# Four feed forwards: the fourth-quarter sums of the crossed norm moved behind VectorE's second plain multiplication, and T2 kept in the norm's own row

## What is computed

```python
def swiglu(h, w_in, w_out):
    g, u = jnp.split(h @ w_in, 2, axis=-1)
    return (jax.nn.silu(g) * u) @ w_out

h = h + g2 * swiglu(modulate(h, norm2_g[l], sh2, sc2), ffn_w_in[l], ffn_w_out[l])   # first block
x = layer_norm(ALPHA * x + g_f * swiglu_2(h, ffn_w1[i], ffn_w3[i], ffn_w2[i]), ...)  # second block
```

## Time and profile before

| | before |
|---|---|
| median of three runs | 4000.85 us |
| the profiled execution, its own time | 4003.02 us |
| its span, first to last instruction | 4000.9 us |
| TensorE matmuls busy | 3700.5 us (92%) |
| VectorE, ScalarE, GpSimd busy | 2337.9, 1505.0, 1802.7 us |
| mean granted TensorE clock | 0.947 of full speed |

### The profile page before, as it was taken

One profiled execution on the slowest core, in us unless ns is written; L12 is line 12 of the kernel. 1 busy time (PEld: TensorE's weight loads), 2 busy tenths in 40 slices (PEclk: granted clock), 3 DMA queues, 4 the chain that ended last, 5 costly groups with the idle time before them and its releaser, 6 DMA issues. The chain is left out here.

```text
span 4000.9 us, 82113 instructions
## 1 busy us (share of the span) xinstructions
PE 3700.5 (92%) x33646; PEld 3242.0 (81%) x33646; DVE 2337.9 (58%) x4324; ACT 1505.0 (38%) x2826; POOL 1802.7 (45%) x1226
## 2 busy tenths in 40 slices
PE   6998899999899899989799999979999999988997
PEld 5877799999677788868698888769999878668996
DVE  3345566666553766685557775276666640637665
ACT  3235333333365443332234443243333241644443
POOL 2201455554344777632233432155555332737884
PEclk8999999999999999989879999889999989989998
DMA  4223233332201444432201100223333211012331
GB/s 177 69 98 106 90 101 112 119 108 95 70 5 48 152 154 154 137 112 109 76 20 31 29 21 25 80 85 106 106 116 114 72 63 64 23 54 74 101 101 63
DMA packets 159555, 343.99 MB, mean 86 GB/s; under 512 B 33487, under 2 KB 89295, under 8 KB 158799
## 3 DMA queue, kind: packets, MB, share of 16 engines
q1 hardware_dynamic: 139311, 266.37, 20.2%
q10 hardware_dynamic: 19872, 72.36, 5.3%
HBM read 323.88 MB, written 16.93 MB: 85 GB/s over the span
## 5 line engine op out<-in xcount | busy, mean ns | idle before, releaser
L1450 POOL TENSOR_TENSOR feed_low<-feed_sums,feed_high 128x512 fp32r<-128x512 f32 x320 | 502.0, 1587 | 476.0 <-ACT feed_high L1444 468.0
L1450 POOL TENSOR_TENSOR feed_low<-ring,feed_high 128x512 fp32r<-128x512 f32 x448 | 596.2, 1347 | 193.6 <-ACT feed_high L1444 96.7
L1444 ACT ACTIVATE feed_high<-ring 128x512 fp32r<-128x512 f32 x448 | 278.5, 626 | 433.2 <-PE ps L1692 243.2
L1676 PE MATMUL ps<-hn_high,feed_high 128*128 128x384 f32 (+1 forms) x1280 | 401.9, 314 | 0.8 <-ACT feed_gate L1764 0.8
L1677 PE MATMUL ps<-hn_low,feed_high 128*128 128x384 f32 (+1 forms) x1280 | 395.4, 309 | 0.0
L1678 PE MATMUL ps<-hn_high,feed_low 128*128 128x384 f32 (+1 forms) x1280 | 395.3, 309 | 0.0
L1690 PE MATMUL ps<-feed_hid,feed_high 128*128 128x384 f32 (+1 forms) x1056 | 378.8, 359 | 13.6 <-DVE h L1874 6.1
L1691 PE MATMUL ps<-feed_hid,feed_high 128*128 128x384 f32 (+1 forms) x1056 | 375.9, 356 | 0.0
L1692 PE MATMUL ps<-feed_hid,feed_low 128*128 128x384 f32 (+1 forms) x1056 | 375.5, 356 | 0.0
L1444 ACT ACTIVATE feed_high<-feed_sums 128x512 fp32r<-128x512 f32 x320 | 189.3, 626 | 488.5 <-DVE feed_sums L1469 275.0
L1676 PE MATMUL ps<-cross_high,feed_high 128*128 128x384 f32 (+1 forms) x960 | 300.3, 313 | 22.7 <-issue 21.7
(11 more groups left out here) (639 smaller groups left out, 9489.1 us busy)
## 6 DMA issues: line engine op xcount, KB each, us to landing
feed_side_ring<-in_ada ACTq DMA_DIRECT2D x138, 512.0 KB, 4.3
ring<-in_ffn_g SPq DMA_DIRECT2D x88, 512.0 KB, 4.9
ring<-in_ffn_u SPq DMA_DIRECT2D x88, 512.0 KB, 3.7
ring<-in_ffn_d SPq DMA_DIRECT2D x88, 512.0 KB, 3.8
diff_side_ring<-in_ada SPq DMA_DIRECT2D x32, 512.0 KB, 4.2
ring<-in_od_in SPq DMA_DIRECT2D x24, 512.0 KB, 4.0
ring<-in_ev_in SPq DMA_DIRECT2D x23, 512.0 KB, 5.2
ring<-in_even_in SPq DMA_DIRECT2D x20, 512.0 KB, 4.1
```

The lines of the kernel that those rows point to most:

```text
L1444: act.activation(self.high[:, e % self.SLOTS, :], self.source(name, n), ACT.Copy).then_inc(self.high_ready, 1)
L1450: pool.tensor_tensor(self.low[:, slot, :], self.source(name, n), self.high[:, slot, :].bitcast(F32), ALU.subtract).then_inc(self.low_ready, 1)
L1676: pe.matmul(dst, high, vh, start=c == 0, stop=False)
```

## The change

In `cross`, T2 is written in place into the second half of its `norm_sq` row in place of `cross_raw`, and `crossed` now counts with T2. For c = 0 and 2 VectorE first waits for GpSimd's low part of norm row c + 4. The two drains behind T2 are gone. The four fourth-quarter sums are a method of their own, `add_fourth`; VectorE calls them after `plain_multiply(1)`, which has moved ahead of `put_low(0)`. They count in a new semaphore. `high_cross` and `low_cross` are two instructions each, one for T1 and T3, one for T2. On ScalarE, `high_fourth` waits for the four sums and stands, with `put_hidden(0)` behind it, after `first_copy` of chunk 2; `put_hidden(0)` now also waits for all four `cross_low`. A wait of ScalarE for a22 of chunk 1 is gone.

```diff
@@ class CrossedStream, cross @@
-        t1, t2, t3 = (self.k.cross_raw[:, j, c, :] for j in range(3))
+        t1, t2, t3 = self.k.cross_raw[:, 0, c, :], lower[:, h:self.tokens], self.k.cross_raw[:, 2, c, :]
...
         if shifted:
-            dve.tensor_tensor(t2, lower[:, h:self.tokens], t1, ALU.subtract)
-            dve.drain()
-            dve.tensor_tensor(self.fourth[:, c, :], lower[:, 0:h], t2, ALU.subtract).then_inc(self.crossed, 1)
+            dve.wait_ge(self.low_pool, self.by_pool.index(c + 4) + 1)
+            dve.tensor_tensor(t2, t2, t1, ALU.subtract).then_inc(self.crossed, 1)
         else:
             for a, b, s in self.second_half():
...
-            dve.drain()
-            dve.scalar_tensor_tensor(out=self.fourth[:, c, :], in0=lower[:, 0:h], scalar=self.shifts[:, c + 4, 0:1],
-                                     in1=t2, op0=ALU.add, op1=ALU.subtract).then_inc(self.crossed, 1)
-        dve.drain()
+            ins.then_inc(self.crossed, 1)
+
+    def add_fourth(self, dve, c):
+        h, lower, t2 = self.half, self.sq[:, c, :], self.sq[:, c, self.half:self.tokens]
+        if c + 4 in self.by_pool:
+            ins = dve.tensor_tensor(self.fourth[:, c, :], lower[:, 0:h], t2, ALU.subtract)
+        else:
+            ins = dve.scalar_tensor_tensor(out=self.fourth[:, c, :], in0=lower[:, 0:h], scalar=self.shifts[:, c + 4, 0:1],
+                                           in1=t2, op0=ALU.add, op1=ALU.subtract)
+        ins.then_inc(self.fourth_raw, 1)
 
     def high_cross(self, act, c):
-        act.activation(self.k.cross[0][:, :, c, :], self.k.cross_raw[:, :, c, :], ACT.Copy).then_inc(self.cross_high, 1)
+        act.activation(high[:, 0:3:2, c, :], raw[:, 0:3:2, c, :], ACT.Copy)
+        act.activation(high[:, 1, c, :], self.sq[:, c, self.half:self.tokens], ACT.Copy).then_inc(self.cross_high, 1)
 
     def low_cross(self, pool, c):
-        pool.tensor_tensor(low, self.k.cross_raw[:, :, c, :], high.bitcast(F32), ALU.subtract).then_inc(self.cross_low, 1)
+        pool.tensor_tensor(low[:, 0:3:2, :], self.k.cross_raw[:, 0:3:2, c, :], high[:, 0:3:2, :].bitcast(F32), ALU.subtract)
+        pool.tensor_tensor(low[:, 1, :], self.sq[:, c, self.half:self.tokens], high[:, 1, :].bitcast(F32), ALU.subtract).then_inc(self.cross_low, 1)
 
     def high_fourth(self, act):
+        act.wait_ge(self.fourth_raw, 4)
...
@@ feed_forward, scalar: put_hidden @@
                 if n == 0:
-                    act.wait_ge(norm.crossed, 4)
+                    act.wait_ge(norm.fourth_raw, 4)
+                    act.wait_ge(norm.cross_low, 4)
@@ feed_forward, scalar: order @@
             norm.high_cross(act, 3)
-            put_hidden(0)
             following("a21", 1)
             following("a22", 1)
-            operands.wait_product(act, "a22", 1)
+            first_copy(PLAIN)
+            side_tiles(4)
             norm.high_fourth(act)
-            side_tiles(4)
-            first_copy(PLAIN)
+            put_hidden(0)
@@ feed_forward, vector: order @@
+            plain_multiply(1)
+            dve.drain()
+            for c in range(4):
+                norm.add_fourth(dve, c)
             put_low(0)
-            plain_multiply(1)
             dve.drain()
             lower_left(PLAIN)
```

More of the change, by code:

```diff
@@ L1312, in __init__ @@
         self.crossed, self.cross_high, self.cross_low = st.sem("norm_crossed"), st.sem("norm_cross_high"), st.sem("norm_cross_low")
+        self.fourth_raw = st.sem("norm_fourth_raw")
         self.fourth_high, self.fourth_low = st.sem("norm_fourth_high"), st.sem("norm_fourth_low")
```

5 lines of the change are left out of this document (3 added, 2 removed).

## The result

The changed kernel takes 3984.23 us, median of 6 runs (3982.75 to 3990.21), against 4001.94 us for the kernel before in the same series. The ratio is 0.995, with a 95% interval of 0.9928 to 0.9972, so 11 to 29 us less. The forecast was 3991.6 us, its range ended at 3987.5: the direction was right, the gain was nearly twice what I forecast. The same program in a second series gave 3987.87 us (6 runs), ratio 0.9956, interval 0.9939 to 0.9974; that median would have lain just inside the forecast's range. From 2100 to 2300 us, in code that no kernel here touches, two of the 14 profiles show a granted clock of 0.82 and last some 20 us longer, where eleven show 0.94 to 0.97 and one 0.89.

A forecast was written before the change was run, and what follows sets the result against it. TensorE was taken as the bound, standing idle ahead of four first crossed products. Gains of 2.9 + 1.4 + 2.9 + 3.3 = 10.5 us, less 0.3 each, made 9.3 us less: 3991.6 us, range 3987.5 to 4000.0.

The forecast's parts named there:

- What bounds s2: TensorE's idle time ahead of the first crossed product, 21.7 us over four feed forwards; two conditions release it.
- the bank: Ahead of s2, first feed forward: the second plain multiplication on VectorE, behind put_low(0), is the last condition by 1.7 us.
- s2 in the four: First crossed product: start at 505.5 in the first feed forward; idle about 2.8, 0, 2.7 and 5 us ahead.
- The sums' place: Four fourth-quarter sums and eight drains leave VectorE's road to s2: crossed 3.3 us earlier, s2 3.9 us.
- the halves: high_cross and low_cross as two instructions each: 1.2 us in place of 1.16, and 2.8 in place of 2.62.
- The row behind: Behind s2: late sums and put_low(0), held by low_fourth, delay the side pair; second idle time 2.9 us.
- the first rival: Clock falls ahead of the side pair, 1.9 us lost in first and third each, unless already fallen ahead of s2; chance 0.20.
- The rival of probability 0.20: Clock falls in the second idle time, ahead of the side pair: 5.5 us less in all, 3995.3 us; chance 0.20.
- From here on the head start stays.: From a12 of chunk 3 order and waits are as before; the first feed forward keeps 2.9 us.
- 10.5 walked: Sum over four feed forwards, walking the queues instruction by instruction: 2.9 + 1.4 + 2.9 + 3.3 us less.
- 0.3 us off each: Deduction from each feed forward's gain because the walk ran early by 0 to 0.9 us; leaves 9.3 us.
- my rule of one at each boundary: VectorE instructions with all operands in SBUF wait for GpSimd's running instruction; one slips in at each boundary.

The follow-up runs named there:

- second pair: Both kernels run and profiled again with nothing changed: kernel before 4002.55 us (8 runs), changed kernel 3987.87 us (6 runs).
- mult_first: Kernel before with only plain_multiply(1) moved ahead of put_low(0) on VectorE: 3999.02 us, ratio 0.9994.
- sums_back_plus120: Changed kernel with the four fourth-quarter sums back inside cross, each behind a drain, and 120 drains added at VectorE's start: 3987.56 us.
- after_plus12: Changed kernel with 12 more drains at VectorE's start, where it is idle: 3995.22 us, ratio 0.9984.

## Why the prediction was wrong in size

**The step that failed** is one that the prediction didn't write down: that all code outside the feed forwards takes what it took. It forecast 9.3 us less, all in the feed forwards. They gave 11.0 (10.7 in the second pair), within 2 of it; the stretch to L3407 gave 6.0 in the first pair of profiles, 4.6 of it up to the pooling's first product. The change has no instruction there. It shortens VectorE's stream, and an idle time that comes at multiples of 128 instructions left a place where 0.44 us cost 4.6.

How much of the measured 17.7 us this explains is open in part. In the second pair the hold was shorter, so that the pooling's first product gained 1.6 us and the whole stretch 0.3. The medians lie 17.7 us apart in the first series and 14.4 in the second (4002.30, all runs of the kernel before there, and 3987.87), 6.7 and 3.7 more than the feed forwards gave. How this rest is shared between the hold and the scatter of the other stages is not shown.

Point by point:

- **What bounds s2.** Right: the bank, by 1.7 us, then the crossed sums (mult_first: 3.25 us left of 4.94). But most of the gain, 6.7 of 11.0 us, comes with this one line alone; I gave the sums and drains the larger part of the work.
- **s2 in the four.** 505.5 was forecast in the first and 504.20 + 1.35 = 505.55 measured; idle 2.2, 0, 2.2 and 4.9 us for 2.8, 0, 2.7 and 5. The last to end is `cross_low`'s second half, as said.
- **The sums' place.** I took 3.3 us of earlier `crossed`, from the sums and the drains together, as 3.3 us of earlier s2, less the halves. Of this the sums' place is worth 0.6 us at s2 in the first feed forward, and at a11 of chunk 3 it costs 2.4 (sums_back_plus120). I had walked that cost, an idle time of 2.9 us, but had not asked whether the order without it would be faster.
- **The row behind.** Right in its mechanism: the last three sums took 2.18, 1.34 and 1.64 us, `put_low(0)` 3.63, and it ended 0.8 us behind `low_fourth`; the side pair started after 2.73 us idle for the 2.9 forecast. In the third it was 1.16, which I had set equal to the first, but the side pair starts as long behind s2 as there (9.22 us for 9.25): the slower clock behind s2 filled the rest, as the first rival says for that case.
- **The clock.** The rival of probability 0.20 came true in the first: 0.66 behind the side pair, which takes 1.74 us for 1.07. In the third the clock was 0.67 behind s2, in the second 1.00 behind the side pair. Along with it the head start fell from 4.2 us at s2 to 2.3 at a12 of chunk 3 in the first.
- **"From here on the head start stays."** Wrong. In the third, 4.7 us at a11 of chunk 3 became 1.6 behind the start of the down products, since the down products wait for VectorE's residual units (3.20 us for 2.04, and the granted clock is 0.66 in the 5 us behind). And 1.1 to 1.2 us came back in the first and third far behind, at the multiplication that takes 1.25 us in place of 2.00, which is the shift's doing and not the edit's. The two about cancel, so that the sum was right to 0.5 us (10.5 walked, 11.0 measured) is luck in part.
- **0.3 us off each** for the walk's error, 1.2 in all, was a correction in the wrong direction.

The Trainium skill (SBUF — State Buffer, "SBUF: two separate sides") has the pair of ports held for a whole instruction. The rows of `put_low(0)` agree (3.63 us when `low_fourth` is running, 0.96 when it runs ahead of it), and L878, which reads one tensor from SBUF, was held as well; the page doesn't say who is next at the end of one. In the rows of the feed forwards shown here VectorE was; L878 was not, twice (5.31 us) or once (3.33), so my rule of one at each boundary doesn't hold everywhere. The Trainium skill (TensorE: Matmul & The Clock Gate, "Part 1: The HAM clock gate") has the slow state as the default. The rows here don't show which idle time is long enough for it: behind 2.73 us and, in the third, 2.21 it fell, and behind 2.21 us in the first feed forward of the changed kernel again, 2.00 and, before, 2.89 it did not.

## What to carry to other kernels

Ask of each wait what stood ahead of the last event on its own queue: one line that lets an instruction with no reason to wait pass one that has to brought more than the four sums that the change is named after. An equal idle time ahead of an instruction doesn't mean an equal start: count from a common point. Measure a part by the durations of that part in two profiles, not by the whole time: the feed forwards repeat to 0.3 us for one program where its whole runs scatter over 7 us and more. And before a gain is credited to an edit, look where an untouched stage changed too, and pad the stream by some instructions to see whether it is the edit or its length.

## What the runs showed of the hardware

- VectorE stands idle for 0.42 to 0.54 us, with nothing to wait for, at places an exact multiple of 128 instructions apart, drains and waits counted: 125 times in 14 profiles. Twelve drains at the start of the program decided whether it stood at one place 1700 us later. The Trainium skill (Perfetto Trace Analysis, "The 4-stage abstract model") has an instruction at 64 bytes. By that figure I estimate 128 of them at 8 KB, which is the size of the smaller pieces in the queues named "instruction". That these idle times are the loading of code is argued from this, not shown.
- A 0.35 us instruction that starts 0.01 to 0.02 us behind one of GpSimd can take 5.31 us, through three of GpSimd's instructions, two of them memsets.
- After an idle time of 2.96 us ahead of the same products the clock was 1.00 in the changed kernel, 0.52 in the same kernel with other memsets 1900 us earlier, and 0.50 for 10 us in after_plus12.
